# First block's causal attention: scores from float32r high and low parts laid on the two row halves, and an earlier load of the distances

## The reference

```
s = einsum(q, k) * 64**-0.5              # 512 x 512 per head, float32
p = masked_softmax(s - slope_h * dist, dist >= 0)
o = g0 * o_cmp + g1 * (p_slc @ v_slc) + g2 * (p_win @ v_win)
```

## Time and profile before

| what | us |
|---|---|
| median of 3 executions | 3386.72 |
| lowest and highest | 3381.82, 3387.19 |
| profiled execution, its own time | 3386.27 |
| profiled execution, its span | 3384.5 |
| PE busy | 3290.4 (97%) |
| DVE busy | 1759.3 (52%) |
| ACT busy | 1298.7 (38%) |
| POOL busy | 212.3 (6%) |
| share of the chain that ended last, PE | 90% |
| of it, L985 (scores of both blocks) | 4% |

### The profile page before, as it was taken

The page is one execution under the profiler, slowest core; times in us unless marked ns, Lnnn a source line. Parts: engine busy times, 40 slices in busy tenths (PEclk is TensorE's granted clock), DMA queues, the critical chain, the costliest instruction groups (busy, mean ns, idle before and its releaser), DMA issues.

```text
span 3384.5 us, 41352 instructions
## 1 busy us (share of the span) xinstructions
PE 3290.4 (97%) x15399; PEld 2631.6 (78%) x15399; DVE 1759.3 (52%) x2614; ACT 1298.7 (38%) x1849; POOL 212.3 (6%) x234
## 2 busy tenths in 40 slices
PE   8989998999999999999999999999999999999998
PEld 6667876888888888875688888878887668888887
DVE  7354478445553455435666555345553566555532
ACT  4226656223332333223256333333332325733322
POOL 1001100000000000000110100010000011010000
PEclk9959999999999999999999999999999999999999
DMA  5220022333333333333122333333333322233332
GB/s 126 88 57 4 1 57 75 100 94 93 99 94 94 98 93 93 98 89 83 51 52 67 90 99 98 92 91 105 93 93 95 81 57 46 64 94 93 99 92 64
DMA packets 518250, 275.12 MB, mean 81 GB/s; under 512 B 39523, under 2 KB 510408, under 8 KB 517987
## 3 DMA queue, kind: packets, MB, share of 16 engines
q1 hardware_dynamic: 513154, 262.77, 28.1%
q0 software_dynamic: 3600, 9.85, 1.1%
q10 hardware_dynamic: 1360, 0.66, 0.1%
HBM read 262.70 MB, written 2.14 MB: 78 GB/s over the span
## 4 chain that ended last, share of the span: by engine, by line
PE 90%; DVE 6%; ACT 2%; issue 1%; DMA 0%; DVEq 0%; POOL 0%; ACTq 0%; POOLq 0%
PE bank L375 25%; PE bank L376 24%; PE bank L377 24%; PE bank L1004 5%; PE bank L985 4%; PE bank L993 3%; PE bank L2392 1%; DVE wlo L351 1%; PE bank L2375 1%; PE bank L1688 1%; PE bank L2362 1%; DVE xc L1894 0%; DVE q L932 0%; PE bank L690 0%; PE bank L1707 0%
## 5 line engine op out<-in xcount | busy, mean ns | idle before, releaser
L375 PE MATMUL bank<-hhi,whi 128*128 128x512 f32 (+1 forms) x2504 | 991.9, 396 | 8.0 <-DVE wlo L351 5.0
L377 PE MATMUL bank<-hlo,whi 128*128 128x512 f32 (+1 forms) x2504 | 977.1, 390 | 0.0
L376 PE MATMUL bank<-hhi,wlo 128*128 128x512 f32 (+1 forms) x2504 | 977.0, 390 | 0.0
L351 DVE TENSOR_TENSOR wlo<-raw,whi 128x1024 fp32r<-128x1024 f32 x485 | 608.8, 1257 | 587.8 <-ACT whi L344 578.9
L344 ACT CAST whi<-raw 128x1024 fp32r<-128x1024 f32 x485 | 505.1, 1046 | 409.1 <-PE bank L377 394.8
L375 PEld LDWEIGHTS bank<-hhi,whi 128*128 128x128 f32 (+1 forms) x2504 | 470.5, 188 | 149.5 <-issue 45.1
L377 PEld LDWEIGHTS bank<-hlo,whi 128*128 128x128 f32 (+1 forms) x2504 | 470.4, 188 | 100.7
L376 PEld LDWEIGHTS bank<-hhi,wlo 128*128 128x128 f32 (+1 forms) x2504 | 470.6, 188 | 99.2 <-issue 3.4
L375 PE MATMUL bank<-uhi,whi 128*128 128x512 f32 x880 | 348.5, 396 | 0.0
L376 PE MATMUL bank<-uhi,wlo 128*128 128x512 f32 x880 | 348.0, 395 | 0.0
L377 PE MATMUL bank<-ulo,whi 128*128 128x512 f32 x880 | 348.0, 395 | 0.0
(11 more groups left out here) (447 smaller groups left out, 3598.8 us busy)
## 6 DMA issues: line engine op xcount, KB each, us to landing
raw<-in_ffn_w_gate SPq DMA_DIRECT2D x88, 512.0 KB, 3.9
raw<-in_ffn_w_up SPq DMA_DIRECT2D x88, 512.0 KB, 3.8
raw<-in_w_in SPq DMA_DIRECT2D x78, 512.0 KB, 3.8
raw<-in_ffn_w_down SPq DMA_DIRECT2D x64, 512.0 KB, 4.1
raw<-in_w_out SPq DMA_DIRECT2D x24, 512.0 KB, 4.1
raw<-in_ffn_w_down SPq DMA_DIRECT2D x32, 384.0 KB, 3.5
raw<-in_w_gate SPq DMA_DIRECT2D x22, 512.0 KB, 4.0
raw<-in_w_up SPq DMA_DIRECT2D x22, 512.0 KB, 3.8
```

The costliest lines, as they stand in the source:

```text
L351: k.nc.vector.tensor_tensor(k.wlo[:, slot, :], k.raw[:, slot, :], k.whi[:, slot, :].bitcast(F32), ALU.subtract)\
L375: mm(out, whi, hi(kc), start=start and i == 0, stop=False)
L376: mm(out, wlo, hi(kc), start=False, stop=False)
L377: last = mm(out, whi, lo(kc), start=False, stop=stop and i == kcs - 1)
```

## The change

`first_norms` and `q`: `q` becomes 128 partitions x 8 chunks x 512, two heads to a chunk, one in each half. The zeroing by POOL goes away, and each chunk of queries is one DVE instruction of 128 partitions. So that the scores of `compressed_attention` stay right, `kcmp` is written only in the partition half that belongs to its group (the rest is zero from an earlier memset), as two instructions of 64 partitions.

`dist` is allocated with `q` and loaded by POOL behind `cmpmask`, one stage sooner; POOL no longer waits for it in front of the causal attention.

`causal_attention`: the scores become two float32r matmuls per step. The stationary operand is `stacked`: one half of the partitions holds the high part of the head's queries, the other half the low part. The moving operand is `keys`: the high part of the keys in both halves for the first matmul, the low part in both halves for the second. The DVE makes all of these: per head a copy and a subtraction of 64 x 512, per pair of group and branch (8 pairs) two copies and two subtractions of 64 x 512. Each copy is followed by a wait of the DVE on itself. Where they stand: before step 0 the keys of (group 0, first branch) and head 0; behind step 0 the keys of (group 0, second branch) and head 1; then keys behind steps 32g+3 and 32g+11 for group g+1, and head h+1 behind step 8h.

```
--- before
+++ after
@@ normalize
-            for a, b, part in it.get("parts", [(0, rows, out)]):
-                last = nc.vector.scalar_tensor_tensor(out=part, in0=it["src"][a:b], scalar=it["gain"][a:b],
-                                                      in1=k.bank[5 - i % 2][a:b, :], op0=ALU.mult, op1=ALU.mult)
-            last.then_inc(*k.xn_done.up())
+            nc.vector.scalar_tensor_tensor(out=out, in0=it["src"], scalar=it["gain"], in1=k.bank[5 - i % 2][0:rows, :],
+                                           op0=ALU.mult, op1=ALU.mult).then_inc(*k.xn_done.up())
@@ attention, ACT's list
+        if on_act:
+            on_act(act, -1)
@@ first_block
-                q = sb("q", [P, NH, T], F32, q_mem)
+                q, dist = sb("q", [P, KC, T], F32, q_mem), sb("dist", [P, T], F32, q_mem)
...
+                    pool.dma_start(dist[:, :], k.consts["dist"]).then_inc(*k.stage_landed.up(by=16))
@@
+def query_rows(h):
+    g = h // HPG
+    return slice(HD * (g % 2), HD * (g % 2) + HD), g // 2 * HPG + h % HPG
@@ first_norms
-    @k.block.gpsimd
-    def _(pool):
-        for c in range(0, NH, HPG):
-            r = 64 * (1 - c // HPG % 2)
-            pool.memset(q[r:r + HD, c:c + HPG, :], 0.0).then_inc(*k.q_zero.up())
...
+    items = [dict(norm=c, rows=P, src=raw_queries(otok, c), out=q[:, c, :], gain=gain) for c in range(KC)]
@@ causal_attention
-    @k.block.gpsimd
-    def _(pool):
-        pool.dma_start(dist[:, :], k.consts["dist"]).then_inc(*k.stage_landed.up(by=16))
-        pool.wait_ge(*k.stage_landed.all())
+    stacked, keys = sb("qparts", [P, 2, T], F32R), sb("kparts", [P, 2, 2, 2, T], F32R)
...
-                steps=[dict(pairs=[(q[:, h, t * P:(t + 1) * P], kT[:, 2 * b + g // 2, 0:(t + 1) * P])],
+                steps=[dict(pairs=[(stacked[:, h % 2, t * P:(t + 1) * P], keys[:, g % 2, b, e, 0:(t + 1) * P])
+                                   for e in range(2)],
...
-    attention(k, groups, mem, builds)
+    other = lambda rows: slice(HD - rows.start, P - rows.start)
+    head_at = {8 * h: h + 1 for h in range(NH - 1)}
+    head_at[-1] = 0
+    keys_at = {32 * g + 3 + 8 * b: (g + 1, b) for g in range(NG - 1) for b in range(2)}
+    keys_at.update({-1: (0, 0), 0: (0, 1)})
+    order = [keys_at[t] for t in sorted(keys_at)]
+    ready = {8 * h: [k.q_parts.at(h + 1)] for h in range(NH)}
+    for g in range(NG):
+        for b in range(2):
+            ready.setdefault(32 * g + 4 * b, []).append(k.k_parts.at(order.index((g, b)) + 1))
+
+    def both_parts(dve, t):
+        if t in keys_at:
+            g, b = keys_at[t]
+            rows, _ = query_rows(HPG * g)
+            src, hi, lo = kT[rows, 2 * b + g // 2, :], keys[:, g % 2, b, 0, :], keys[:, g % 2, b, 1, :]
+            if g >= 2:
+                dve.wait_ge(*k.qk_done.at(32 * (g - 1)))
+            for to in (rows, other(rows)):
+                last = nc.vector.tensor_copy(hi[to], src)
+            last.then_inc(*k.k_high.up())
+            dve.wait_ge(*k.k_high.at(order.index((g, b)) + 1))
+            for to in (rows, other(rows)):
+                last = nc.vector.tensor_tensor(lo[to], src, hi[rows].bitcast(F32), ALU.subtract)
+            last.then_inc(*k.k_parts.up())
+        if t in head_at:
+            h = head_at[t]
+            rows, c = query_rows(h)
+            if h >= 2:
+                dve.wait_ge(*k.qk_done.at(8 * (h - 1)))
+            nc.vector.tensor_copy(stacked[rows, h % 2, :], q[rows, c, :]).then_inc(*k.q_high.up())
+            dve.wait_ge(*k.q_high.at(h + 1))
+            nc.vector.tensor_tensor(stacked[other(rows), h % 2, :], q[rows, c, :], stacked[rows, h % 2, :].bitcast(F32),
+                                    ALU.subtract).then_inc(*k.q_parts.up())
+
+    attention(k, groups, mem, builds, ready=ready, splits=both_parts)
@@ compress
-        nc.vector.scalar_tensor_tensor(out=kcmp[:, :, 0:NCMP].rearrange("p g n -> p n g"), in0=by_block(kraw),
...
+        for e in range(2):
+            rows = slice(HD * e, HD * e + HD)
+            nc.vector.scalar_tensor_tensor(out=kcmp[rows, e::2, 0:NCMP].rearrange("p g n -> p n g"),
...
@@ compressed_attention
-                last = nc.tensor.matmul(k.bank[t % 2][:, 32 * h:32 * h + 32], q[:, h, t * P:(t + 1) * P],
+                last = nc.tensor.matmul(k.bank[t % 2][:, 32 * h:32 * h + 32], q[:, query_rows(h)[1], t * P:(t + 1) * P],
```

More of the change, by code:

```diff
@@ L1375, in first_block @@
             with ExitStack() as mem:
-                causal_attention(k, mem, q, kT, vals, gates, otok)
+                causal_attention(k, mem, q, dist, kT, vals, gates, otok)
                 outputs = k.pt_copied.all(), k.o_read.all(), k.o_added.all()
@@ L1463, in first_norms, with causal_attention @@
     normalize(k, items, back, *scales[1:], NORM1_HEADS)
-def causal_attention(k, mem, q, kT, vals, gates, otok):
+def causal_attention(k, mem, q, dist, kT, vals, gates, otok):
     nc = k.nc
-    sb = lambda name, shape: mem.enter_context(nc.sbuf_tensor(k.name(name), shape, F32))
-    dist, bias = sb("dist", [P, T]), sb("bias", [P, 2, T])
-    @k.block.gpsimd
-    def _(pool):
-        pool.dma_start(dist[:, :], k.consts["dist"]).then_inc(*k.stage_landed.up(by=16))
-        pool.wait_ge(*k.stage_landed.all())
+    sb = lambda name, shape, dt=F32: mem.enter_context(nc.sbuf_tensor(k.name(name), shape, dt))
+    bias = sb("bias", [P, 2, T])
+    stacked, keys = sb("qparts", [P, 2, T], F32R), sb("kparts", [P, 2, 2, 2, T], F32R)
     handover(k)
@@ L1661, in _ @@
         by_block = lambda t: t[:, 0:cols].rearrange("p (n g) -> p n g", g=NG)
-        nc.vector.scalar_tensor_tensor(out=kcmp[:, :, 0:NCMP].rearrange("p g n -> p n g"), in0=by_block(kraw),
-                                       scalar=vector(k, "k_norm_g")[:, 0:1], in1=by_block(kroot), op0=ALU.mult,
-                                       op1=ALU.mult)
+        for e in range(2):
+            rows = slice(HD * e, HD * e + HD)
+            nc.vector.scalar_tensor_tensor(out=kcmp[rows, e::2, 0:NCMP].rearrange("p g n -> p n g"),
+                                           in0=by_block(kraw)[rows, :, e::2], scalar=vector(k, "k_norm_g")[rows, 0:1],
+                                           in1=by_block(kroot)[rows, :, e::2], op0=ALU.mult, op1=ALU.mult)
         dve.wait_ge(*k.cmp_v.at(1))
@@ L2827, in build @@
         k.latent_hi = signal("latent_hi")
+        k.q_high, k.q_parts, k.k_high, k.k_parts = (signal(n) for n in ("q_high", "q_parts", "k_high", "k_parts"))
         k.x_odd, k.vt_copied, k.t5_landed = signal("x_odd"), signal("vt_copied"), signal("t5_landed")
```

## The result

The changed kernel took 3356.53 us (median of 4, 3352.83 to 3358.95) against 3384.27 us for the kernel before, measured beside it (median of 4). The ratio is 0.9917, 95% interval 0.9905 to 0.9929: 24 to 32 us faster. Two further rounds gave 0.9923 (0.9909 to 0.9936) and 0.9914 (0.9900 to 0.9929). The forecast was 3364 us with a range from 3357 to 3375.

What follows compares the result with a forecast made beforehand. PE was taken to set the pace of the causal attention. Scores -22.0, norms -3.4, start +0.3, clock +2.0 and lumps +0.5 gave -22.6 us from 3386.27, so 3364 us, range 3357 to 3375.

Steps and rivals of the forecast that it cites:

- What bounds the kernel, and that no engine takes over: Causal attention: PE, busy 178.36 of 178.70 us, sets the pace; ACT and DVE can follow a 4.75 us period.
- The rest, 3.12 us, is transposes and values, which the change leaves alone: Causal attention: of PE's 5.49 us group period, the 3.12 us outside the scores was held constant.
- 0.10 + 2 x 0.105 = 0.31: Causal attention, 128-key scores: fixed 0.10 us plus a 0.105 us floor for each of two float32r matmuls.
- 0.74 us saved a group: Causal attention: scores fall from 2.37 to 1.63 us a group, -22.0 us over 29.75 groups.
- the allowance for stretched lumps: Causal attention: DVE's part-making may lengthen now and then where POOL adds tiles; 0.5 us added in all.
- 1.11 each: Queries' norms: whole-chunk DVE instructions at 1.11 us an interval, 11 intervals, saving 3.4 us.
- The start: Start of causal attention: dist's load leaves the chain, DVE's first parts replace it; +0.3 us, plus 2.0 for a later clock rise.
- The fill: Causal attention, first score to transposes of step 4: forecast +1.9 us, from DVE's parts and a later clock rise.
- Loads exposed: Rival, causal scores: each float32r matmul pays 0.105 us for its weight load, 10 us less gain, 3374; chance 0.10.
- DVE or ACT paces: Rival, causal attention: DVE lumps or ACT's uneven steps hold the period at 5.1 us, 3374; chance 0.10.
- Better (3358): Rival, causal attention: 128-key pairs at 0.21 us, no clock loss, lumps free; 3358 us; chance 0.07.
- Slower by the clock: Rival, causal attention: PE stays at 1.2 GHz; about 3403 us if for half the stage; chance 0.03.

Runs made afterwards that it cites:

- the float32 control: Changed kernel with one float32 matmul per score over the dense 128 rows (heads summed, no parts made): 3375.51 us, 0.9974 of the kernel before.

## Why the prediction was off

**What bounds the kernel, and that no engine takes over: right.** PE pays the same price for each group from the fourth on, and the DVE's lumps are free. That was argued from the DVE's lead of three steps; the run with doubled subtractions shows both that it holds and where it ends.

**"The rest, 3.12 us, is transposes and values, which the change leaves alone": wrong, and the step that failed.** The rest became 3.03, 2.7 us less over 29.75 groups. In the float32 control the value records in front of the scores take 0.84 us for eight, in the changed kernel 0.82 (medians 0.841 and 0.813), and likewise by 0.03 at each of the four steps; the one transpose behind the 128-key scores gives back 0.02. I had counted a matmul group from its own start to the next group's, and so had put the cost of changing over to float32 scores on neighbours that I then held constant.

**"0.10 + 2 x 0.105 = 0.31" for 128 keys: too dear, and the second term that failed.** It measured 0.26; 0.33, 0.44 and 0.55 measured 0.32, 0.44 and 0.55. The floor itself, borrowed from float32 records of 65 columns, was right for the second matmul, which adds 0.11 us. What failed was to put the fixed 0.10 on top of two floors: the first matmul took 0.14 alone. So the term "0.74 us saved a group" measured 5.49 - 4.58 = 0.91. The new period is 4.58 to 4.59, not 4.75, and 0.16 x 29.75 = 4.8 us of the missing 5.4 in that line of the table come from it; 0.5 is the allowance for stretched lumps, which was not needed: the parts' longest instructions in the changed kernel were 426 and 690 ns.

**"1.11 each" for the norms: 1.01 on the average.** One of the three intervals of the earlier trace rows was the change from halves to wholes, and was longer than the other two. 11 x 0.1 = 1.1 us.

**The start: the sum right, a term of it off.** The second handover cost less than I had taken, so the first score came 0.2 us nearer instead of 0.4 us farther. The fill was forecast at +1.9 and measured at +1.9. Of its two named causes the clock is seen in the trace: it rises after 11.2 us of broken work instead of 4.6. That the numbers agree is partly luck: in the kernel with the norms in halves, where it rose after 8.5 us, the same fill was 1.0 us shorter. How the rest splits between the clock and the parts behind step 0, no run shows.

The errors have one sign: -4.8 - 0.5 - 1.1 - 0.6 = -7.0. With the 1.9 us of the compressed attention's clock and the 4.4 us given back behind the stage, which are scatter, the profiled spans differ by 27.3 us; the forecast was 22.6.

**Rivals.** Loads exposed: fell. The Trainium skill (TensorE: Matmul & The Clock Gate, The mechanism) has weight loads hidden only when the row group differs; here both matmuls of a pair load all 128 rows, and the second adds 0.12 us at 256 keys, where its columns alone take 0.11; only at 128 keys does it add more than its columns. DVE or ACT paces: fell at this size; the exponential shows up at a period of 4.18. Better (3358): nearest in number, 1.5 us off, but not in mechanism. Of its three terms only the free lumps came; the 128-key pair took 0.26 us and not 0.21, and the clock's loss at the start was there. The term that made up for them, the cheaper neighbours, is in no rival. Slower by the clock: did not happen, because the change fills all 128 rows. I had given it 0.03 for a stage "with a third less columns"; in the runs it hung on the rows of the scores, which the forecast had not considered.

## What to carry to other kernels

When one engine paces a pipeline, read the period of the whole group in a kernel or stage that already has the new form, not the price of the new instruction beside "unchanged" neighbours; and leave an interval out of an average if it spans a change of form. A load taken out of the chain is worth only what does not move into its place: here the DVE's first parts took all of it, and one more move, to where the DVE idles a stage earlier, brought another 4.5 us by the medians of one round and 7.9 by the stages. Before a microsecond at the start of a stage is put down to an edit, compare when the clock rose in both runs. Before splitting a 128-row matmul into a 64-row one to save masking, look at the granted clock of a run.

## What the runs showed of the hardware that I had not expected

With scores over 64 rows, in float32 or in float32r, the causal attention ran at 1.2 GHz for 382 of its 386 us and 323 of its 324 us, with PE busy over 99% of it. The clock rose once only the last transposes and values were left, about 8 and 9 us after the start of the last score. With the same matmuls over 128 rows it was at 2.4 GHz from the start in float32, and after 11.2 us in float32r. The transposes and the values were the same in all of them. The 64-row form also cost about 0.38 us a step beside the clock. A float32r pair shortens the float32 group in front of it by 0.03 us. And the second float32r matmul of a pair adds 0.11 us at 128 columns and 0.12 at 256: below 256 columns less work did not make it shorter.
